# A transformer layer with a 16-expert mixture on one core: the first expert's preparation moved into the ranking stage, semaphores cleared one stage later

## The reference, cut to what matters

```python
def ec_moe(h, w_router, w_g, w_u, w_d):
    B, n, D = h.shape
    cap = EC_FACTOR * n // N_EXPERTS          # 256 sample tokens, 32 prompt tokens for each of 16 experts
    aff = jax.nn.softmax((h @ w_router).astype(jnp.float32), axis=-1)
    vals, idx = lax.top_k(aff.transpose(0, 2, 1), cap)
    xg = jax.vmap(lambda hb, ib: hb[ib])(h, idx)
    a = jnp.einsum('becd,edf->becf', xg, w_g)
    u = jnp.einsum('becd,edf->becf', xg, w_u)
    y = jnp.einsum('becf,efd->becd', jax.nn.silu(a) * u, w_d) * vals[..., None].astype(h.dtype)
    return jax.vmap(lambda ib, yb: jnp.zeros((n, D), yb.dtype).at[ib.reshape(-1)].add(yb.reshape(-1, D)))(idx, y)
```

## Time and profile before

| | |
|---|---|
| median of 3 runs | 3092.93 us (3091.52 to 3095.8) |
| profiled execution, its own time | 3096.9 us |
| span of the profiled execution | 3095.1 us |
| PE, DVE, ACT, POOL busy | 94%, 64%, 35%, 34% |
| last count of the ranking's rounds to first expert product (PE L2430 at 2321.68, L2931 at 2348.51) | 26.8 us |

### The profile page before, as it was taken

The page is one execution under the profiler, slowest core; times in us unless marked ns, Lnnn a source line. Parts: engine busy times, 40 slices in busy tenths (PEclk is TensorE's granted clock), DMA queues, the critical chain, the costliest instruction groups (busy, mean ns, idle before and its releaser), DMA issues. The chain is left out here.

```text
span 3095.1 us, 42645 instructions
## 1 busy us (share of the span) xinstructions
PE 2902.2 (94%) x16270; PEld 2285.7 (74%) x16270; DVE 1982.5 (64%) x2559; ACT 1086.6 (35%) x1723; POOL 1066.6 (34%) x690
## 2 busy tenths in 40 slices
PE   6999999999789999999999999989957999999993
PEld 3888888888666666666666667878846888888882
DVE  5418292829448888888878866555684566566665
ACT  5311111111344444444444443223423333433334
POOL 1000000000114343444433545521117765656652
PEclk8999999999888999999999999999978999999996
DMA  6313222311540110110110126565425666666657
GB/s 233 101 50 107 79 101 86 107 64 55 176 153 22 27 33 7 34 32 13 27 27 7 59 80 224 175 240 189 159 86 170 189 204 202 190 204 207 203 184 289
DMA packets 139519, 371.25 MB, mean 120 GB/s; under 512 B 20886, under 2 KB 47996, under 8 KB 129116
## 3 DMA queue, kind: packets, MB, share of 16 engines
q1 hardware_dynamic: 99756, 266.55, 25.7%
q0 software_dynamic: 24048, 74.72, 8.8%
q10 hardware_dynamic: 15552, 27.79, 2.5%
HBM read 266.07 MB, written 102.89 MB: 119 GB/s over the span
## 5 line engine op out<-in xcount | busy, mean ns | idle before, releaser
L1188 ACT ACTIVATE at_w<-banks 128x512 f32<-128x512 f32 (+1 forms) x592 | 347.7, 591 | 464.5 <-PE banks L1294 409.2
L1410 DVE TENSOR_REDUCE at_mpart<-banks 128x1 f32<-128x512 f32 (+1 forms) x584 | 373.4, 681 | 138.2 <-PE banks L1321 138.1
L1266 POOL TENSOR_TENSOR at_part<-at_part,at_w 128x512 f32<-128x512 f32 x224 | 298.1, 1331 | 326.8 <-ACT at_w L1188 323.5
L2637 POOL TENSOR_TENSOR moe_gu_lo<-raw,moe_gu_hi 128x2048 fp32r<-128x2048 f32 x63 | 293.7, 4667 | 108.5 <-ACT moe_gu_hi L2705 108.1
L517 DVE SCALAR_TENSOR_TENSOR fr_r<-fr_r,fr_dw 128x2334 f32<-128x2334 f32 x120 | 318.0, 2650 | 3.9
L374 PE MATMUL fr_po<-hT_hi,fr_w_hi 128*128 128x512 f32 (+1 forms) x800 | 296.8, 371 | 3.0 <-PE fr_po L374 1.8
L374 PE MATMUL fr_po<-hT_lo,fr_w_hi 128*128 128x512 f32 (+1 forms) x800 | 294.6, 368 | 0.0
L374 PE MATMUL fr_po<-hT_hi,fr_w_lo 128*128 128x512 f32 (+1 forms) x800 | 294.5, 368 | 0.0
L1332 PE MATMUL banks<-at_w,V 128*64 128x256 f32 (+1 forms) x2368 | 283.0, 381 | 0.0
L2837 DVE TENSOR_TENSOR moe_d_lo<-moe_raw_d,moe_d_hi 128x1024 fp32r<-128x1024 f32 x64 | 190.7, 2980 | 102.6 <-ACT moe_d_hi L2746 102.6
L1436 DVE TENSOR_TENSOR at_part<-at_part,at_w 128x512 f32<-128x512 f32 x224 | 231.4, 1033 | 13.0
(11 more groups left out here) (409 smaller groups left out, 6745.6 us busy)
## 6 DMA issues: line engine op xcount, KB each, us to landing
raw<-w_gate_up SPq DMA_DIRECT2D x64, 1024.0 KB, 4.8
moe_raw_d<-w_down SPq DMA_DIRECT2D x64, 512.0 KB, 5.1
fr_wm<-w_ada_rows POOLq DMA_DIRECT2D x32, 512.0 KB, 4.6
gates_scratch<-fr_r ACTq DMA_DIRECT2D x64, 256.0 KB, 2.0
mx_gates<-gates_scratch SPq DMA_DIRECT2D x64, 256.0 KB, 3.0
fr_raw<-w_in SPq DMA_DIRECT2D x28, 512.0 KB, 5.4
fr_r<-x POOLq DMA_DIRECT2D x18, 512.0 KB, 5.6
raw<-mixed_scratch SPq DMA_DIRECT2D x9, 1024.0 KB, 6.1
```

What stands on the lines that cost most here:

```text
L1188: act.activation(w[:, g % NW, k, 0:n], sc[:, (2 * g + k) % SCB, 0:n], ACT.Exp, scale=SM_SCALE).then_inc(exp_done, 1)
L1266: pool.tensor_tensor(part[:, j % 2, 1, 0:n], before, w[:, g % NW, 1, 0:n], ALU.add).then_inc(add_p, 1)
L1410: dve.tensor_reduce(mpart[:, s, tiles, c // 2], bank, AX.X, ALU.max).then_inc(red_done, 1)
L2637: pool.tensor_tensor(gu_lo[:, slot], raw_gu[:, slot], gu_hi[:, slot].bitcast(F32), ALU.subtract).then_inc(glo_done, 1)
```

## The change

1. **Semaphores.** `Scope.zero_sems` and its blocks are gone. A new object `Phases` keeps the semaphores of the present stage and of the one before; POOL clears those of the stage before as its first instructions in the next stage's block (`phases.clear`). One block at the very end clears the last ones.
2. **The first expert's weights.** SP issues the first two `w_gate_up` loads between the last list loads and pair `LAST`'s stores. ACT makes `gu_hi` of both pieces in `out_phase` as soon as the output projection is done (into the room of its second half of weights), and POOL makes `gu_lo` in four halves behind its last `shifted`. SP then loads the four `w_down` pieces, each behind one half. DVE's split of piece 0 (L2823) and POOL's of piece 1 are gone from `moe_phase`.
3. **The search.** A copy of `bits`, `digits`, is put into PSUM ahead of the first round and L2316 reads it. `token_numbers` moves from round 8 to 10, the affinities from 9 to 10; prompt sort rounds 0 and 1 move to rounds 12 and 13, rounds 2 and 3, `prompt_lists` and `tab_prompt` behind `pos`.
4. **The first look-up.** POOL issues `look_up(0)` in `out_phase`, as soon as `pos` is there.
5. **The first expert's start.** `keep_busy(13)` in place of 10, and `keep_busy(3)` behind the turns of the first and of the third part. SP loads pieces 2 and 3 one after the other (each waits for the one before), and only then the gates.

```diff
-        ctx.callback(self.zero_sems)
+    def begin(self):
+        self.last.close()
+        self.last, self.now = self.now, self.last
+        self.to_clear, self.used = self.used, []
...
+        digits = po[:, 0, 2 * E:2 * E + 4 * ROUNDS].bitcast(U32).rearrange("p (r c) -> p r c", c=4)
...
                         load_lists(QUARTERS - 1, range(LISTS // 2, LISTS, 2))
+                        for q in range(2):
+                            sp.wait_ge(m_lo_done, PAIRS - 2 + q)
+                            sp.dma_start(raw_gu[:, q], t["w_gate_up"][q]).then_inc(first.gu_ld[q], 16)
...
-                for q in range(2):
-                    sp.wait_ge(m_lo_done, PAIRS - 2 + q)
-                    sp.dma_start(raw[:, q * 2 * D:(q + 1) * 2 * D].rearrange("p (g k n) -> p g k n", g=2, k=KD),
-                                 t["w_gate_up"][q]).then_inc(gu_ld[q], 16)
+                for m in range(FF // P):
+                    sp.wait_ge(first.glo_done, m + 1)
+                    sp.dma_start(raw_d[:, m], t["w_down"][m * P:(m + 1) * P, :]).then_inc(first.d_ld[m], 16)
...
                 copy_h(2 * LAST, LAST, 0)
+                act.wait_ge(mm_done, 2 * PAIRS)
+                for q in range(2):
+                    act.wait_ge(first.gu_ld[q], 16)
+                    act.activation(gu_hi[:, q], raw_gu[:, q], ACT.Copy).then_inc(first.ghi_done, 1)
...
                 shifted(2 * LAST + 1, 1, 1)
+                for q in range(2):
+                    pool.wait_ge(first.ghi_done, q + 1)
+                    for g in range(2):
+                        pool.tensor_tensor(gu_lo[:, q, g], raw_gu[:, q, g], gu_hi[:, q, g].bitcast(F32), ALU.subtract
+                                           ).then_inc(first.glo_done, 1)
+                pool.wait_ge(tab_done, 1)
+                pool.wait_ge(list_st, 16 * QUARTERS)
+                pool.wait_ge(tail, 14)
+                for i in range(2):
+                    pool.indirect_dma_start(tab[:, 0, i], None, t["ranked"], bass.IndirectOffsetOnAxis(ap=pos[:, i, 0:1], axis=0)
+                                            ).then_inc(first.tab_ld, 16)
...
-                beside[8] = [lambda: largest(LAST), token_numbers]
-                beside[9] = [lambda: affinities(LAST)]
-                for n in range(CAPP // 8):
-                    beside[11 + n] = [lambda n=n: prompt_round(n)]
-                beside[14].append(prompt_lists)
+                beside[8] = [lambda: largest(LAST)]
+                beside[9] = []
+                beside[10] = [lambda: affinities(LAST), token_numbers]
+                for n in range(2):
+                    beside[12 + n] = [lambda n=n: prompt_round(n)]
...
+                dve.tensor_copy(digits, bits[:]).then_inc(digits_done, 1)
+                dve.wait_ge(digits_done, 1)
...
-                        dve.tensor_scalar(cand[:], bits[:, r + 1], low[:].bitcast(U32), None, ALU.bitwise_or).then_inc(cand_done, 1)
+                        dve.tensor_scalar(cand[:], digits[:, r + 1], low[:].bitcast(U32), None, ALU.bitwise_or).then_inc(cand_done, 1)
...
                 dve.tensor_tensor(pos[:], place, base[:], ALU.add).then_inc(tail, 1)
+                for n in range(2, CAPP // 8):
+                    prompt_round(n)
+                prompt_lists()
+                tab_prompt()
...
-                look_up(0)
-                pool.sem_inc(looked, 1)
                 gather(0, 0)
                 look_up(1)
-                pool.wait_ge(glo_done, 1)
-                split_gu(1, 1)
                 look_up(2)
                 look_up(3)
...
-                keep_busy(10)
+                keep_busy(13)
                 for i in range(3):
                     pe.wait_ge(xg_ld[i], 16)
                     for half in range(2):
                         turn(0, i, half, 0)
+                    if i != 1:
+                        keep_busy(3)
```

193 lines of the change are left out of this document (113 added, 80 removed).

## The result

| | before | changed |
|---|---|---|
| median of runs, us | 3093.77 (3091.52 to 3095.80, 4 runs) | 3075.55 (3073.80 to 3077.89, 4 runs) |
| ratio to before, 95% interval | 1 | 0.9933 (0.9921 to 0.9945) |
| profiled execution, us | 3096.9, span 3095.1 | 3074.9, span 3073.1 |

By the ratio the change is faster by 20.7 us (17 to 24.4), where I had forecast 13.9; the two medians stand 18.2 apart. Two repeats of the changed kernel further down gave 0.9939 and 0.9936, that is 18.9 and 19.8 us.

The account below looks back on a forecast made before the run. PE sets the pace except in the chain from the last dense product to the first expert's product. Barriers 2.6, earlier first product 7.5 and waits 3.76 sum to 13.9 us: median 3092.93 to 3079.0, range 3074 to 3086.

Parts of the forecast that it names:

- all that follows is work of PE in order: Behind the chain up to the first expert's product: time taken out of that chain leaves the end of the kernel.
- Barriers, 2.6: Four changes of stage: one barrier less saves 0.65 us each, 2.6 in all, bounds 0 to 5.2.
- 0.25 that I charged for POOL's clearing: At the gather in the new stage: POOL alone clears semaphores, costing 0.25 us, bounds 0 and 1.0.
- The search, 4.86: DVE's search rounds up to `pos`: the PSUM operand and moved prompt work gain 4.86 us.
- that rival (0.08): Search rounds 5 to 9: POOL's halves hold DVE's counts by up to 9.2 us; gain 4.7, 3088.2 us; chance 0.08.
- The look-up and the pick, 8.3: Search, early look-up and one barrier less: the pick comes at 2328.8 against 2337.08, 8.3 us earlier.
- The start of the first expert, 0.8 lost: From pick to first expert's product: the longer keep_busy puts it 12.25 us behind the pick against 11.43, 0.8 lost.
- the clock, 0: First expert's first products: the same low clock stretch (3.44 us at 0.50) comes again, 0 gained.
- the rival with 0.17: First expert's start: the clock rises during the longer keep_busy, saving 1.7 us there; gain 15.2, 3077.7 us; chance 0.17.
- PE's waits for `gu_lo`, 3.76: First two experts: POOL's chain starts 4.3 us earlier, so PE's waits of 0.45 and 3.31 both go, 3.76.
- my 1.3 to spare: First two experts: POOL's split ends at 2412.9, PE without waits is there at 2414.2, 1.3 us to spare.
- SP's new order: First expert's loads: pieces 2 and 3 in turn, then gates, land by about 2353, before DVE's work at about 2356.

Follow-up runs that it names:

- x4: The kernel before with the semaphore edit alone (cleared one stage later, one barrier less at each change of stage); ratio to before 0.9962, 11.8 us faster.
- y0: The changed kernel again, nothing edited; ratio to before 0.9939.
- z0: The changed kernel, nothing edited, as reference for the runs beside it; ratio to before 0.9936, median 3075.6 us.
- z1: The changed kernel with ten keep_busy groups instead of 13 and none behind the first and third turned part; ratio to before 0.9942.
- z2: The changed kernel with the four look-up transfers of the sixth piece moved to the seventh; ratio to before 0.9910, median 3070.1 us.
- y1: The changed kernel with the search's L2374 reading its digits from SBUF again, the PSUM copy still made; ratio to before 0.9956.
- y6: The changed kernel with the first expert's first two splits back behind the change of stage, weights still loaded early; ratio to before 0.9957.
- y2: The changed kernel with the first expert's look-up back behind the change of stage; ratio to before 0.9961.
- y5: The changed kernel with the four look-up transfers of the sixth piece moved to the seventh; ratio to before 0.9928.

## Why the prediction was right or wrong

**Wrong: "all that follows is work of PE in order".** This sentence of the first part let me stop reading at the first experts, and the sum had no term for the loop. 7.3 us were there, a third of the whole, PE's ten waits of 0.5 and 0.6, 5.6 together, which the waits view lists in two rows, and some 0.36 a late pass by which PE is busy longer. That they would go could not have been foretold from the trace, since they hang on 0.25 us; that they were there, and that anything could turn them, could. Without them the gain by the three ratios would be 11.6 to 13.4, and the forecast of 13.9 would look nearly exact, but by luck: other terms were off in both directions.

**Barriers, 2.6: right.** 2.5 by the four gaps, in the changed kernel and in x4. The other 2.6 us ahead of `out_phase` can't be given to the change: five traces with the same early stages (the first one, y0, z0, z1, z2) reach it between 2037.2 and 2045.3. Between 800 and 1000 us the granted clock was 0.90 in the earliest (z2) and 0.86 in the latest (z1). The 0.25 that I charged for POOL's clearing was right too: its first gather starts 1.25 behind the pick, was 0.95.

**The search, 4.86: right.** 5.3. Rounds 4, 8 to 11 and 14 gave 1.93, 0.39, 0.11, minus 0.76, 1.01 and 1.77, each as worked out; the step from round 0 to round 1 gave 0.84 and not 0.45. The PSUM operand (y1) and the counts beside POOL's halves (y6) did what I took: that rival (0.08) is out. From the start of `out_phase` to round 0 0.5 was lost, where I had 0.2 for `digits`; its copy takes 0.22.

**The look-up and the pick, 8.3: right.** 7.9 against round 0. Within it the search gave 0.4 more, and the pick is 5.97 behind `pos` (y2: 10.5) where I had 5.2: the look-up is issued 0.9 and not 0.1 behind `pos`, which the barrier hid, and the change of stage takes 1.27 where I took a third of 1.39.

**The start of the first expert, 0.8 lost, and the clock, 0: mis-sized and wrong; the rival with 0.17 was right on the clock.** The first product is 11.63 behind the pick and not 12.25, and 26 instead of 14 products fit in the first 3.45 us. z1 and the first pieces of 6.46 show that the added keep_busy does it. My evidence against it was the 4.59 us of keep_busy at 0.52, and I read it as a clock that gapless products don't raise. Cut where the granted clock changes, the windows of before read otherwise:

```profile
2337.30:2341.71 4.41, 4.41 (x20) 4.34 (x20) 0.00 (x0) 0.00 (x0) 2.77 (x3) 0.50 0.43 124
2341.71:2345.13 3.42, 1.55 (x12) 1.14 (x11) 1.29 (x2) 1.09 (x2) 3.09 (x3) 1.00 0.57 185
2345.13:2348.51 3.38, 2.47 (x17) 2.03 (x15) 1.93 (x5) 1.72 (x4) 3.38 (x1) 0.50 0.71 196
```

The ten groups had raised the clock by their end, and it was lost again over the turns, with the gaps of 0.50 and 1.37 in the earlier trace rows. In the changed kernel it rises at 2330.30, just as near the end of the thirteen groups, and the two times three groups fill those gaps, so it is still there at the first product. They keep the clock; they don't raise it. The Trainium skill (TensorE: Matmul & The Clock Gate, Why this matters for your kernels), which I had set against the row, agrees with z0 and z1. The rival's price was 1.7; z1 loses 2.4 (2.7 by the end of its first piece, 9.12 for 6.46), and 0.6 more ahead of the first product.

**PE's waits for `gu_lo`, 3.76: wrong.** Only 0.45 shrank, to 0.28; 3.31 stayed. The 2.3 us that went between the first product and the loop are the clock (1.5 in the first piece) and shorter waits (0.8), not this term. POOL's start was as forecast: its split of piece 2, the third, starts 21.2 behind the pick and not 25.5, 4.3 earlier. Two things used up my 1.3 to spare. From there to the end of the eighth piece's split POOL takes 65.1 (62.9 before), as four transfers that start beside a `d_lo` now take 1.6 to 1.91. And PE, without the wait, comes to the eighth piece 83.0 behind the pick, where I had 85.4.

An earlier POOL wouldn't have helped either, and there my model was wrong: it had POOL's chain hang on the pick alone. The split of piece 2 starts 0.08 behind the end of ACT's `gu_hi`, which waits for PE's first piece. In z1, where PE's first piece is 2.7 longer, POOL stands idle for it:

```profile
2354.84 4.62 POOL L2705 TENSOR_TENSOR late<-moe_raw_gu,late 128x2048 fp32r<-128x2048 f32 x1 [2.28 <-ACT late L2770]
```

In all 14 traces with the look-ups in their old pieces, before and after, PE waits 0.27 to 0.45 for the split of the sixth piece, so the two stand side by side there. From there POOL takes 25.0 to the end of the eighth piece's split (two splits, a scatter and eight look-up transfers), PE 21.7 for two pieces. The wait is the difference, 3.29 to 3.35, whatever was earlier or later ahead of it (y6, z1). y5 and z2, which take four transfers out of that stretch, remove it.

SP's new order was not covered either. DVE waits for the gates until 2349.37, and the second piece's `hid` is 2.3 late; PE lost nothing by it in this trace, but 2.0 in z2, where `hid` is 4.6 late.

## What to carry to other kernels

Ask the waits view for every stretch behind the change too, and multiply each row by its passes: waits of 0.5 and 0.6, once each in five passes, went with 7.3 us, nearly as much as the whole term of the pick. Where two engines start instructions within 0.1 us of each other and one is held for the other's length, an edit elsewhere can change the kernel's time by flipping their order (x4), so look at the same pair in both traces before crediting the edit. And when PE waits for a helper engine, find what the helper itself last waited for: if that is PE, an earlier start moves both and the wait stays. Then count the work of both from the last place where they met. Last, cut a window where the granted clock changes: the mean of 0.52 hid that the clock had risen in its last stretch and was lost behind it, which called for filled gaps and not for giving the clock up.
